# The low parts of four FFN weight chunks move from VectorE to GpSimd, the norm's sum moves forward in its chunk, the SiLU table is loaded behind the root

## The reference

```
lat = lat + g1 * yl
hl  = modulate(rmsnorm(lat, norm_g[1]), sh2, sc2)
lat = lat + g2 * conv_ffn(hl)

def conv_ffn(h, w_up, conv_w, conv_b, w_down):
    u = dwconv(h @ w_up, conv_w, conv_b)          # 3 taps along the tokens
    gate, val = split(u, 2)                       # 2816 columns each
    return (silu(gate) * val) @ w_down
```

## Time and profile before

| | us |
|---|---|
| median of 3 runs (lowest, highest) | 877.88 (877.25, 877.94) |
| the profiled execution, its own time | 877.51 |
| its span in the trace | 875.7 |
| TensorE busy in the span | 859.7 (98%) |
| VectorE busy | 674.6 (77%) |
| ScalarE busy | 504.0 (58%) |
| GpSimd busy | 48.1 (5%) |

### The profile page before, as it was taken

The page is one execution under the profiler, slowest core; times in us unless marked ns, Lnnn a source line. Parts: engine busy times, 40 slices in busy tenths (PEclk is TensorE's granted clock), DMA queues, the critical chain, the costliest instruction groups (busy, mean ns, idle before and its releaser), DMA issues.

```text
span 875.7 us, 16628 instructions
## 1 busy us (share of the span) xinstructions
PE 859.7 (98%) x6028; PEld 768.4 (88%) x6028; DVE 674.6 (77%) x1155; ACT 504.0 (58%) x819; POOL 48.1 (5%) x19
## 2 busy tenths in 40 slices
PE   8999999999999799999999999999999999999997
PEld 3688888888899799999999899999998888888886
DVE  4783899999998888887787797766577767666665
ACT  5434677777766665666666645555554555444444
POOL 0000000000006425200000000000000000000000
PEclk9999999999999899999999999999999999999999
DMA  9983444444456365665654565444465457555551
GB/s 345 408 297 140 157 141 150 149 146 147 144 177 234 121 241 175 211 197 189 199 191 137 189 197 163 150 161 137 162 203 161 142 182 226 191 184 182 187 189 50
DMA packets 45441, 160.90 MB, mean 184 GB/s; under 512 B 5200, under 2 KB 6608, under 8 KB 45264
## 3 DMA queue, kind: packets, MB, share of 16 engines
q1 hardware_dynamic: 43488, 156.43, 52.4%
q10 hardware_dynamic: 1904, 3.81, 1.2%
HBM read 159.16 MB, written 1.05 MB: 183 GB/s over the span
## 4 chain that ended last, share of the span: by engine, by line
PE 87%; DVE 8%; ACT 2%; DMA 1%; issue 1%; SPq 1%; DVEq 0%; ACTq 0%
PE bank L422 17%; PE bank L423 17%; PE bank L424 16%; PE bank L443 6%; PE bank L487 5%; PE bank L489 5%; PE bank L488 5%; PE bank L444 3%; DVE w_lo L416 3%; PE bank L1251 2%; PE bank L1255 2%; PE bank L1259 2%; DMA arena<-in_ada 1%; ACT w_hi L409 1%; PE bank L1377 1%
## 5 line engine op out<-in xcount | busy, mean ns | idle before, releaser
L416 DVE TENSOR_TENSOR w_lo<-raw,w_hi 128x1024 fp32r<-128x1024 f32 x244 | 302.6, 1247 | 107.6 <-ACT w_hi L409 107.3
L409 ACT ACTIVATE w_hi<-raw 128x1024 fp32r<-128x1024 f32 x244 | 253.5, 1051 | 78.7 <-PE bank L424 36.6
L422 PE MATMUL bank<-h_both,w_hi 128*128 128x256 f32 (+2 forms) x928 | 282.8, 305 | 3.1 <-DVE arena L2081 2.2
L423 PE MATMUL bank<-h_both,w_hi 128*128 128x256 f32 (+2 forms) x928 | 277.2, 299 | 0.0
L424 PE MATMUL bank<-h_both,w_lo 128*128 128x256 f32 (+2 forms) x928 | 277.2, 299 | 0.0
L422 PEld LDWEIGHTS bank<-h_both,w_hi 128*128 128x128 f32 x928 | 175.9, 190 | 11.9 <-DVE arena L2081 2.4
L423 PEld LDWEIGHTS bank<-h_both,w_hi 128*128 128x128 f32 x928 | 176.3, 190 | 5.3
L424 PEld LDWEIGHTS bank<-h_both,w_lo 128*128 128x128 f32 x928 | 175.5, 189 | 5.7
L422 PE MATMUL bank<-y_hi,w_hi 128*128 128x256 f32 x304 | 87.7, 289 | 2.6 <-DVE w_lo L416 2.5
L424 PE MATMUL bank<-y_hi,w_lo 128*128 128x256 f32 x304 | 86.4, 284 | 0.0
L423 PE MATMUL bank<-y_lo,w_hi 128*128 128x256 f32 x304 | 86.3, 284 | 0.0
(11 more groups left out here) (290 smaller groups left out, 1267.3 us busy)
## 6 DMA issues: line engine op xcount, KB each, us to landing
raw<-in_stream SPq DMA_DIRECT2D x244, 512.0 KB, 3.3
arena<-in_ada SPq DMA_DIRECT2D x40, 512.0 KB, 7.3
xres<-in_ada SPq DMA_DIRECT2D x8, 512.0 KB, 3.4
tok<-in_tok SPq DMA_DIRECT2D x4, 512.0 KB, 5.5
con<-in_con ACTq DMA_DIRECT2D x1, 1472.0 KB, 6.1
xres<-in_tok ACTq DMA_DIRECT2D x1, 1024.0 KB, 8.8
out<-arena SPq DMA_DIRECT2D x4, 256.0 KB, 2.0
arena<-in_post_mix ACTq DMA_DIRECT2D x1, 512.0 KB, 4.3
```

Source lines behind the costliest of these rows:

```text
L409: act.activation(w_hi[c.slot][:, :], raw[c.slot][:, :], ACT.Copy).then_inc(S("split_hi"), 1)
L416: dve.tensor_tensor(w_lo[c.slot][:, :], raw[c.slot][:, :], w_hi[c.slot][:, :].bitcast(F32), ALU.subtract).then_inc(S("split_lo"), 1)
L422: pe.matmul(dst, hi_w, a_hi, start=start, stop=False, skip_group_check=True)
L423: pe.matmul(dst, hi_w, a_lo, start=False, stop=False, skip_group_check=True)
```

## The change

- GpSimd makes the low parts of the FFN's chunks 2 to 5, ahead of its work on the gate row; VectorE no longer makes them and goes straight from the input's low parts to `add_squares`. The two places where the engine that makes the low parts changes get a wait for the counter of low parts, so that it counts in order.
- `squares_sum` stands behind piece 2 of chunk 3 (nine matmuls) instead of piece 4 (fifteen).
- ScalarE loads the SiLU table directly behind the root.
- `ffn_up` waits for one scaled half ahead of its first chunk and for the second ahead of its second, instead of for both ahead of the first.

```diff
@@ lo
             dve.wait_ge(S("split_hi"), c.n + 1)
+            if c.least in (N_FFN + 2, N_FFN + 6):
+                dve.wait_ge(S("split_lo"), c.n)
             dve.tensor_tensor(w_lo[c.slot][:, :], raw[c.slot][:, :], w_hi[c.slot][:, :].bitcast(F32),
@@ scalar
             norm_rstd(act, 0, 1, bank=3, dst=rstd[:, 1:1 + T])
+            act.preload_act_table_set("silu_and_others")
@@ tensor
-            column_tile(pe, Chunk(N_FFN, 3), psum[7][:, 0:FW], FW, FW, lambda: squares_sum(pe, 3), KT // 2)
+            column_tile(pe, Chunk(N_FFN, 3), psum[7][:, 0:FW], FW, FW, lambda: squares_sum(pe, 3), 2)
             def ffn_up(j, p, c):
+                pe.wait_ge(S("z"), j * 2 - 3)
+                column_tile(pe, c[0], psum[4 + p][:, 0:FW], FW, FW)
                 pe.wait_ge(S("z"), j * 2 - 2)
-                column_tile(pe, c[0], psum[4 + p][:, 0:FW], FW, FW)
                 column_tile(pe, c[1], psum[6 + p][:, 0:FW], FW, FW)
@@ gpsimd
+            for k in range(2, 6):
+                lo(pool, Chunk(N_FFN, k))
             for k in range(KT):
                 pool.wait_ge(S(f"mod_loaded{k % 4}"), 16 * (k // 4 + 3))
@@ vector
-            for k in range(2, 6):
-                lo(dve, Chunk(N_FFN, k))
-                if k == 3:
-                    add_squares(dve)
+            add_squares(dve)
             dve.memset(rstd[:, 0:FW:FW - 1], 1.0).then_inc(S("final_weights"), 1)
```

## The result

The changed kernel takes 881.51 us (median of 11 runs, 878.39 to 882.88), the kernel before on the same chip 877.88 (11 runs, 877.16 to 878.25). The ratio of the two is 1.0036, with a 95% interval of 1.0022 to 1.005 (the two medians alone give 1.0041): slower, by 3.6 us between the medians, where the prediction had 2.0. The eleven times lie in two groups, four from 878.39 to 879.19 and seven from 881.33 to 882.88. The profiled execution is one of the upper group (882.25 us, span 880.5), 4.8 us above the span before.

What follows compares the result with a forecast made beforehand. TensorE was busy 98% of the span, its waits traced to VectorE, which GpSimd holds up. Terms -2.4 + 2.6 + 1.8 = +2.0 on 877.88 gave 879.9 us; range 875.0 to 884.0.

Steps and rivals of the forecast that it cites:

- VectorE and GpSimd hold each other up: Both engines: a GpSimd add meeting VectorE costs it up to 2.1 us, a GpSimd product up to 0.8.
- Low part of chunk 2: GpSimd, from 270.1 to 272.6 us: covered by VectorE's line 621, cost 0.
- slower by more: Rival, chance 0.17: GpSimd's first add itself takes 4.6 us longer, delaying the start; +5.4, 883.3 us.
- Low part of chunk 3: GpSimd, ready from 274.6 us: breaks into VectorE's line 605 and holds it 2.1 us.
- Adds: VectorE's seven adds start at 278.3, chunk 4's low part holds the seventh; end at 282.9, 0.9 us sooner.
- The sum's place and the split wait: TensorE: sum after nine matmuls of chunk 3 worth 0.5 us; waiting by scaled halves taken as 0.
- Table load: ScalarE, directly behind the root: ends at 285.9 us and costs 0.8 before its next work.
- Root and first scaling: Behind the adds: root 0.9 us sooner, line 2081 at 284.6, 2.4 sooner; TensorE's 2.2 us wait goes.
- Tile 0 and chunk 6: VectorE, from 287.1 us: one product and one add meet it; chunk 6's low part ends at 295.4, gain 2.4.
- What is late next: From 295 to 304 us: two products and two adds, 5.8 us, meet VectorE; 2.6 us of waiting left.
- Last four gate rows: GpSimd's rows from 315.94 us: up to 2.9 us each for VectorE, 0.8 regained per tile; 1.8 us charged.
- if the sum stands later than 283.85, towards slower: Sign on TensorE: a sum of squares starting after 283.85 us would show the forecast wrong towards slower.

Runs made afterwards that it cites:

- the low parts alone: Changed kernel with table load, sum's place and up product's wait put back as before, leaving only the four low parts on GpSimd: 882.17 us.
- the kernel with the adds kept clear: Changed kernel, with GpSimd making the low parts of chunks 3 to 5 only when the seven adds are done: 879.23 us.
- the spread-out row: Kernel before, with the gate row's eight loads spread over the FFN: 877.12 us; the same edit in the changed kernel: 879.89 us.
- the fastest kernel here: Changed kernel with gate row and chunk 3 on VectorE, chunk 2 on GpSimd beside the residual, 4 and 5 behind the adds, no early table load: 868.31 us.
- the changed kernel with the short row: Changed kernel with GpSimd's gate-row products and adds cut from 1024 columns to 8: 873.35 us.

## Why the prediction was right or wrong, point by point

The direction and the range held; the mechanism (VectorE and GpSimd hold each other up) is the one that decided, but at another place than the forecast put it. That the sum came near is luck: in the profiled run the start, restart included, cost 3.9 us where it was to gain 2.4, and what follows it cost 0.9 instead of 4.4.

- **Low part of chunk 2: right.** It ran beside line 623 in 2.41 us and cost 0, also by itself. With that the rival "slower by more" falls: GpSimd's first add shows no 4.6 us of its own. The Trainium skill ("GPSIMD Engine Reference", section "2.1 Instruction dispatch") names about 6 us for the first call of a freshly loaded kernel; it has them as a gap without an instruction in the profile. Neither shows here: GpSimd's first two-input instruction starts within 0.1 us of the high part it waits for (which ends at 269.16 plus 1.06 in this profile) and takes 2.41; whether it was freshly loaded isn't known.
- **Low part of chunk 3: the step that failed.** I let it break into line 607, as a product had done before, and charged 2.1 us there. It got its turn among the adds instead, and the prediction's next step, "Adds", let only chunk 4 in, at the seventh. In fact chunks 3, 4 and 5 held three adds in a row for 2.2 us each and the first product held a fourth for 0.8: 7.3 us (9.89 less the free 2.56). The adds ended at 286.10, not 282.9. For chunk 4 I had gone by the one add at 276.54, which waited long for its turn. The trace after shows the other pattern: chunk 3's low part let six pass, and chunks 4 and 5, right behind it, none.
- **The sum's place and the split wait: worth nothing.** Predicted were 0.5 and 0. Without the low parts they bring nothing that can be told (878.23, with the table load in it), as the prediction said of the place alone. In the changed kernel the adds came too late for the place to matter: TensorE stood 4.5 us at the sum in its new place, 3.8 in its old one (the low parts alone).
- **Table load: 0.8 us on the path, right in the profile** (the bias starts at 289.55, the first scaling ended its first half at 288.75). In the times it can't be told from nothing.
- **Root and first scaling.** Predicted at 284.6, measured 288.32: 3.2 us of the adds, and 0.5 more, most of it in TensorE's two sums, which are slow behind the wait (1.12 us for the two, 0.70 before).
- **Tile 0 and chunk 6.** I had one product and one add meet it, 2.9 us. It was two adds and two products, 4.6 us (1.93 + 0.86 in line 2091, 1.59 in line 2108, 0.24 in chunk 6's low part). So the start went from the predicted -2.4 to +3.1, and the slow restart added 0.8, which I had not charged beyond the one before.
- **What is late next: 2.6 predicted, 0.3 measured** (chunk 9 starts 4.2 us later than before, chunk 7 3.9), and that 0.3 isn't a wait: the first three matmuls of chunk 7 are still slow, 0.21 us apart. TensorE came some 5.5 us later than forecast, so the low parts of chunks 7 and 8 were ready. Where the start is free, in the kernel with the adds kept clear, waits of this kind do appear (1.4 us ahead of chunk 7 and 2.1 ahead of chunk 8).
- **Last four gate rows: 1.8 predicted, 0.6 measured** (the span's 4.8 less 4.2; one wait of 0.6 is listed, at 353 us). The margin that was to refill by 0.8 per tile didn't save the spread-out row either.

The terms of the profiled run: 3.1 + 0.8 + 0.3 + 0.6 = 4.8, against -2.4 + 2.6 + 1.8 = 2.0. The sentence "if the sum stands later than 283.85, towards slower" was the right alarm: it stood at 286.15. Open is why a GpSimd add lets eight instructions of VectorE pass in one profile, six in another and none in a third.

## What to carry over

Before moving work to an idle engine, ask whether the two can run side by side at all, and price the move by what the busy engine loses. Here a two-input low part that costs VectorE 1.2 us itself cost it 2.2 as GpSimd's where it met an add, and the gate row, taken back from GpSimd, made the kernel 9 us faster. The Trainium skill says so too ("Perfetto Trace Analysis", section "Optimizing Scalar/DVE Operations": moving work between those two might not help); what GpSimd does keep should lie beside instructions that read a PSUM bank, or in a pause of VectorE, as in the fastest kernel here.

## What was not expected of the hardware

- GpSimd's low parts and VectorE's adds alternated one for one: three adds of 2.56 to 2.62 us in a row, against 0.42 alone, while a row of eight instructions of line 607 ran at its free pace (3.26 us) with a GpSimd low part already begun.
- 48 us of GpSimd work held VectorE for 13.6 us, and 9.7 us of VectorE did the same work (the page's busy times with and without it).
- Behind the wait of 4.9 us TensorE had a granted clock of 0.50 for the whole window from 300 to 305 us, and chunk 6 took 5.26 us; behind the 2.5 us wait of before it took 4.43, and behind the 0.6 of the changed kernel with the short row 2.96. So the longer wait came with 0.8 us beyond its own length.
